# One load of layer 0's projection weights for both token streams, own slots for the first modulation weights, a reordered output projection and new placement spans, in an eight-core diffusion backbone

## The chip, the cores and the metric

The kernel runs on all 8 cores of one Trainium2 chip. Each core works alone on its own batch share (two prompt sequences of 256 tokens and one sample of 1024 tokens); there is no exchange between the cores. The metric is the device time in microseconds (us) of the slowest core.

## What is computed

Four layers, each an attention block and an MLP, are applied to two streams that use the same weights. Per layer `l` and stream:

```
m  = silu(c) @ ada_w[l] + ada_b[l]              # six modulation vectors: sh1 sc1 g1 sh2 sc2 g2
h  = rms_norm(y, norm1_g[l]) * (1 + sc1) + sh1
even l: bg,cg,xa,q,k,v = split(h @ even_w_in)   # 1024 -> 3072
        a   = bg * short_conv(cg * xa)          # width 3 over positions
        att = attention(rms(q), rms(k), v)      # prompt: dense in 256 tokens;
                                                # sample: 2-D neighbourhood + 256 cached keys
odd l:  pooling (short window means) and latent attention (q and kv through low-rank maps)
y += g1 * (concat(a, att) @ w_out)
h  = rms_norm(y, norm2_g[l]) * (1 + sc2) + sh2
y += g2 * (relu(h @ w1)**2 @ w2)                # 1024 -> 4096 -> 1024
```

Outputs are both streams and the prompt's keys, values and latent states of every layer.

## The kernel before, in words

**Layout.** `yT` (float32) and `hT` (bfloat16) hold the 1536 tokens of a core transposed: channels on partitions, tokens in three blocks of 512. Block 0 is the prompt (`GP`, P), blocks 1 and 2 the sample (`GS`, S). All weights lie in device memory as float32 tiles of 128 x 2048 (8 x 256 columns) and are cast to bfloat16 by the DMA that loads them; such a DMA is issued by GpSimd (`wtile`, L813). The page gives its bfloat16 size, 512 KB; 1.05 MB are read. A tile goes into one of the six slots of `WC`, but for the sample's MLP, which has a ring of four slots of its own in the arena (`WB` in `mlp`).

**Stages.** For every layer and stream the program has a group of operations: `aP0` and `aS0` are the attention blocks of prompt and sample in layer 0 (`even_attn`, L1277, or `odd_attn`, L990), `mP0` and `mS0` the MLPs (L894), `adaA` and `adaB` the modulation products (`ada_part`, L839: 8 tiles for shift 1 and scale 1, 16 tiles for the rest). `adaB`'s four closing vector operations wait for all its 16 tiles, and every later update of `yT` reads their result. `norm` (L875) squares 8 chunks of a block on ScalarE, sums them with 8 matmuls against `ones`, takes two ScalarE passes for the reciprocal root (tile `RS`), and then runs 8 pairs of a VectorE product (`NT`) and a shift into `hT`. In an even layer a block's projection is `qk_tile` (L1319), 8 matmuls of 512 columns plus one for the norm, 8 times; `v_tile` (L1348), 16 matmuls of 256 columns, 4 times; and `conv` (L1374), three sets of 8 matmuls of 512 columns, 4 times. `even_attn` loads the 12 tiles of `even_w_in` once for P and once more for S.

`out_proj` (L954) runs weight tile by weight tile: for each of the four tiles both sample blocks are multiplied and added into `yT`; after the last tile come the norms of all blocks. `mlp` starts from these norms.

**Order.** The order on the engines is worked out while the program is built. Every operation has a key. `place` (L219) lays the keys of a group along a span of time, by cumulated TensorE work. `schedule` (L237) then plays the program: at each step the engine that can start first takes, among the operations that can start within 0.12 us (TensorE) or 0.04 us (others), the one with the lowest key. Loads into the same set of slots are issued in the order of their keys, each when a slot is free; a matmul that takes a PSUM bank is held until what its readers need from earlier operations has been placed. The engines then run this fixed order and wait on semaphores. The durations used (in `MMG`, `TRG` and `DMA_RATE`, L216, among others) therefore change the order and nothing else.

The spans (L1514 to L1531) set what runs beside what: the MLP of the prompt beside the sample's attention (`mP` with `aS`), and the prompt's attention of the next layer beside the sample's MLP (`aP` with `mS`). Before, the two of a pair end at the same time.

**Arena.** One piece of SBUF is reused by all stages; a new region waits for every reader and writer of what lay there. In layer 0 the sample takes words 0 to 18496, the prompt 19008 on, and for its V, convolution and probability tiles `BZ` (13056) to 16640.

Of the kernel before, what the change touches and what calls it, by code (L numbers as in the profile page):

```python
# [7 lines left out]
BF16 = mybir.dt.bfloat16  # L8
AF = mybir.ActivationFunctionType
ALU = mybir.AluOpType  # L10
# [102 lines left out]
class Prog:  # L113
# [101 lines left out]
    LAT = {"pe": 0.22, "act": 0.12, "dve": 0.10, "pool": 0.12, "sp": 0.1}  # L215
    DMA_RATE = 0.34e6  # L216
    LEAD = 12.0
# [343 lines left out]
def build(depth=4):  # L561
# [37 lines left out]
    with ExitStack() as st:  # L599
# [30 lines left out]

        SZ, BZ, PZ = 19008, 13056, 4608
        ARENA_W = SZ + PZ
        arena = sb("arena", (128, ARENA_W))
# [75 lines left out]
        def MMG(items, reads, writes, key=None):  # L709
            dur = 0.0  # L710
            fns = []
            for it in items:
                out, lhsT, rhs, start, stop = it[:5]
                skip = len(it) > 5 and it[5]
                n = fsize(rhs)
                dur += max(n / 2400.0 + 0.0025, 0.027) + (0.027 if n <= 128 else 0.0)
                fns.append(lambda h, out=out, lhsT=lhsT, rhs=rhs, start=start, stop=stop, skip=skip:
                           h.matmul(R(out), lhsT=R(lhsT), rhs=R(rhs), start=start, stop=stop, skip_group_check=skip))  # L718
            return P.add("pe", fns, reads, writes, dur, key=key)
# [5 lines left out]
        def TRG(items, reads, writes, key=None):  # L725
            fns = [lambda h, o=o, a=a: h.transpose(R(o), R(a), ident[:, :]) for (o, a) in items]  # L726
            P.add("pe", fns, reads + [bid], writes, 0.085 * len(items), key=key)

# [109 lines left out]

        def ada_part(l, part):  # L839

# [3 lines left out]
            for nt in tiles:  # L844
                w = wtile(WC, ada_w[l, nt])
                its = []
                for j in range(2):
                    c = 2 * (nt * 2 + j - n0)
                    for kc in range(8):
                        its.append((pt[:, c:c + 2], w[:, kc, j * 128:(j + 1) * 128], sTb[:, kc, :], kc == 0, kc == 7))  # L850
                MMG(its, [w.b, bsm], [pt.b])
                P.key += 1
            if part == "A":
                pv = pt[:, 0:32].rearrange("p (n m) -> p n m", m=2)
                for m in range(2):
                    TT(mod[:, l, 0:16, m], pv[:, :, m], adab_sb[:, l, 0:16], ALU.add, [pt.b, bsm], [bmodA[l]])
                for m in range(2):
                    STT(A1[:, l, :, m], mod[:, l, 8:16, m], 1.0, n1g_sb[:, l, :], ALU.add, ALU.mult,
                        [bmodA[l], bsm], [bmodA[l]])
            else:  # L860
                pv = pt[:, 0:64].rearrange("p (n m) -> p n m", m=2)
                for m in range(2):
                    TT(mod[:, l, 16:48, m], pv[:, :, m], adab_sb[:, l, 16:48], ALU.add, [pt.b, bsm], [bmodB[l]])
                for m in range(2):
                    STT(A2[:, l, :, m], mod[:, l, 32:40, m], 1.0, n2g_sb[:, l, :], ALU.add, ALU.mult,
                        [bmodB[l], bsm], [bmodB[l]])

        def grid(ap):
# [85 lines left out]
        def out_proj(G, l, wsrc, lo, blo, hi, bhi, K0, zone):  # L954

            for nq in range(4):
                w = wtile(WC, wsrc[nq], key=K0 + nq * 0.1)
                for k, tb in enumerate(G.tbs):
                    for j in range(2):
# [3 lines left out]
                        prs = [(w[:, kc, j * 128:(j + 1) * 128], lo[:, kc, sl] if kc < 4 else hi[:, kc - 4, sl]) for kc in range(8)]  # L963
                        MMK(pt[:], prs, [w.b] + blo[k] + bhi[k], [pt.b], key=K0 + nq * 0.1)
                        STT(yT[:, n, blk(tb)], pt[:], mod[:, l, 16 + n, G.m:G.m + 1], yT[:, n, blk(tb)],
                            ALU.mult, ALU.add, [pt.b, bmodB[l], by[tb][n]], [by[tb][n]], key=K0 + nq * 0.1)
            for k, tb in enumerate(G.tbs):
                norm(G, l, 2, tb, key=K0 + 1 + k * 0.1, zone=zone)

# [20 lines left out]
        def odd_attn(G, l):  # L990
# [284 lines left out]
            out_proj(G, l, owout[i], poolT, bpool, attT, batt, 40, MM5)  # L1275

        def even_attn(G, l):  # L1277
            i = l // 2
            P.key = 0.0
            S = G.name == "S"  # L1280
# [6 lines left out]
            else:  # L1287
                ar, ax = Arena(SZ, SZ + PZ), Arena(BZ, SZ)
            nv = G.nt + (2 if S else 0)
# [14 lines left out]

            Wt = ewin[i]
            if S:
# [53 lines left out]

            wq = [wtile(WC, Wt[2 + n], key=0.1 + n * 0.02) for n in range(2)]
            wv = [wtile(WC, Wt[n], key=0.11 + n * 0.02) for n in range(2)]
            for k in range(nb):
                P.key = 1 + k * 0.1
                for j in range(4):
                    qk_tile(0, k, j, wq[j // 2])
                    v_tile(k * 4 + j, wv)
            wk = [wtile(WC, Wt[4 + n], key=1.15 + n * 0.02) for n in range(2)]
            for k in range(nb):
# [3 lines left out]

            def conv(j, key):  # L1374
                P.key = key
                wa = wtile(WC, Wt[6 + (j // 2) * 3 + j % 2], key=key - 0.5)
                if j % 2 == 0:
                    wbg[0] = wtile(WC, Wt[6 + (j // 2) * 3 + 2], key=key - 0.4)
                wb = wbg[0]
# [23 lines left out]
            if not S:  # L1403
                for j in range(4):
                    conv(j, 10 + j * 2)
                for h in range(8):
                    j = h // 2
# [18 lines left out]
            for j in range(4):  # L1426
                conv(j, 10 + j * 2.0)
            RG = [(0, 8, 0, 4), (0, 12, 0, 0), (4, 16, 1, 0), (8, 16, 1, 0)]
            kvt = lambda c, b: c // 2 * 4 + b * 2 + c % 2
# [44 lines left out]

        spans = {}

        def group(name, fn, *args):
# [4 lines left out]
        def start():  # L1482
# [10 lines left out]
            TS(cv["gqr"], cv["gqr"], float(96 ** -0.5), None, ALU.mult, None, [bsm], [bsm])  # L1493
            for tb in range(3):
                DMA("sp", [(yT[:, :, blk(tb)], xin[:, tb].rearrange("p (c t) -> p c t", c=8))], [], by[tb], "x%d" % tb, key=-2 + tb)
            ada_part(0, "A")
            LOAD("id", [(ident[:], IDd)], [bid], q="pool", key=20)
# [16 lines left out]
        spans["init"] = (-60.0, 0.0)  # L1514
        spans["nS0"] = (0.0, 30.0)
        spans["aP0"] = (1.0, 110.0)
        spans["adaB0"] = (15.0, 75.0)
        t = 20.0
        for l in range(depth):
            la = P.work("aS%d" % l) + P.work("mP%d" % l) + (75.0 if l == 0 else 0.0)  # L1520
            spans["aS%d" % l] = (t, t + la)
            spans["mP%d" % l] = (max(t, 110.0), t + la)
            spans["adaA%d" % (l + 1)] = (max(t, 110.0), t + 0.7 * la + 30)
            t += la
            lb = P.work("mS%d" % l) + (P.work("aP%d" % (l + 1)) if l + 1 < depth else 0.0)
            spans["mS%d" % l] = (t, t + lb)
            spans["aP%d" % (l + 1)] = (t, t + lb)
            spans["adaB%d" % (l + 1)] = (t, t + 0.5 * lb)
# [117 lines left out]
```

How the kernel before makes its waits and increments, by code:

```python
                def body(h):  # L481
                    for waits, fns, inc, every in lst:
                        for s, v in waits:
                            h.wait_ge(s, v)
                        ins = None
                        for n, fn in enumerate(fns):
                            ins = fn(h)
                            if every:
                                ins.then_inc(inc[0], inc[1])
                        if ins is not None and not every:
                            ins.then_inc(inc[0], inc[1])
```

## Time and profile before

| | us |
|---|---|
| median of 3 runs | 2544.39 |
| lowest and highest of them | 2543.35, 2927.85 |
| profiled execution, its own time | 2548.44 |
| span of its slowest core, core 4 (first to last instruction) | 2546.8 |
| spans of the other cores | 2529.6 to 2545.1 |
| TensorE busy in the span | 2332.6 (92%) |
| VectorE, ScalarE, GpSimd busy | 1172.7, 1165.0, 428.4 |

PE is TensorE's matmuls, PEld its weight loads, DVE VectorE, ACT ScalarE, POOL GpSimd, SP SyncE. PEclk is the granted clock as a share of 2.4 GHz. "DMA share" is the mean busy share of the core's 16 DMA engines. In lists of instructions, the bracket gives the idle time of the engine before the piece and what ended it. Matmuls are pipelined: 64 of them in one piece of 14.19 us is 0.22 us each, although one alone is shown with 0.38 us.

### The profile page before, as it was taken

Reading aid. Unit: us, or ns where it says so; the run is one execution under the profiler, and the core shown is the slowest. Engines: PE = TensorE matmul, PEld = TensorE weight load, DVE = VectorE, ACT = ScalarE, POOL = GpSimd, SP = SyncE. Lnnn points to the kernel's source line nnn. Section 1 sums busy time; section 2 is a strip of 40 time slices with the busy share of each in tenths; the row PEclk is TensorE's granted clock in tenths of the full one; section 3 lists DMA queues with packets and bytes.
Section 4 is the critical chain, followed back from the end, with each engine's and each line's share of the span. In section 5 each row is a group of like instructions: output and inputs, shape, how many; then the busy total and the mean of one; then the engine's idle time right before and its main releaser. Section 6 shows DMA issues by size and latency. Waiting matters only on the chain.

```text
span 2546.8 us, 37971 instructions; the slowest of 8 cores (2529.6 to 2546.8 us)
## 1 busy us (share of the span) xinstructions
PE 2332.6 (92%) x12838; PEld 1120.7 (44%) x13082; DVE 1172.7 (46%) x1819; ACT 1165.0 (46%) x2089; POOL 428.4 (17%) x709
## 2 busy tenths in 40 slices
PE   2868989899998999989999899989999899998999
PEld 1533434345543544334444444444554345343444
DVE  1534445544447423353444645545544663335443
ACT  3535553432517488352232546533443466863111
POOL 3211101212103401021120210122111331000000
PEclk8989999899999999989999899999999999998999
DMA  9998878787542654659845377796755155361444
GB/s 193 150 163 138 154 144 142 121 141 131 92 75 51 112 100 75 99 100 156 143 84 108 61 128 145 141 149 116 134 100 94 21 102 86 56 124 34 75 78 113
DMA packets 97035, 281.87 MB, mean 111 GB/s; under 512 B 18896, under 2 KB 28496, under 8 KB 96848
## 3 DMA queue, kind: packets, MB, share of 16 engines
q0 software_dynamic: 76688, 245.17, 58.7%
q1 hardware_dynamic: 20160, 34.25, 4.3%
q8 instruction: 112, 1.84, 0.3%
q14 instruction: 75, 0.61, 0.1%
HBM read 512.85 MB, written 11.67 MB: 206 GB/s over the span
## 4 chain that ended last, share of the span: by engine, by line
PE 78%; DMA 9%; issue 4%; ACT 3%; DVE 3%; POOL 1%; another core or an unknown queue 0%; DVEq 0%; ACTq 0%; POOLq 0%; SPq 0%
PE psall L718 77%; DMA WC<-ada_w 4%; DMA WC<-even_w_in 2%; ACT arena L742 2%; DMA yT<-xin 2%; DVE NT L764 1%; DMA WC<-mlp_w 1%; ACT RS L742 1%; DMA arena<-rpbx 1%; DVE arena L764 1%; POOL RT L753 1%; PE psall L726 0%; DVE arena L753 0%; ACT hT L742 0%; ACT SQ L742 0%
## 5 line engine op out<-in xcount | busy, mean ns | idle before, releaser
L718 PE MATMUL psall<-arena 128*128 128x512 bf16 (+9 forms) x3818 | 804.5, 353 | 17.8 <-DVE arena L753 4.3
L742 ACT ACTIVATE arena<-psall 128x512 bf16<-128x512 f32 (+6 forms) x747 | 420.5, 584 | 660.4 <-PE psall L718 631.6
L718 PE MATMUL psall<-hT,WC 128*128 128x512 bf16 x2534 | 610.5, 386 | 48.7 <-DMA WC<-even_w_in 11.1
L764 DVE SCALAR_TENSOR_TENSOR yT<-psall,mod,yT 128x512 f32<-128x512 f32 x480 | 359.9, 750 | 494.0 <-PE psall L718 485.5
L718 PEld LDWEIGHTS psall<-arena 128*128 128x128 bf16 (+1 forms) x3896 | 356.0, 98 | 410.5 <-issue 69.8
L718 PE MATMUL psall<-hT,arena 128*128 128x512 bf16 x2025 | 469.0, 384 | 11.1 <-ACT hT L742 5.8
L764 DVE SCALAR_TENSOR_TENSOR arena<-psall,arena 128x512 bf16<-128x512 f32 x384 | 264.5, 690 | 417.2 <-ACT arena L742 413.6
L718 PEld LDWEIGHTS psall<-hT,WC 128*128 128x128 bf16 x2608 | 254.1, 99 | 351.3 <-issue 80.2
L718 PE MATMUL psall<-arena,WC 128*128 128x512 bf16 x1378 | 321.7, 380 | 9.5 <-DVE arena L764 2.9
L718 PEld LDWEIGHTS psall<-hT,arena 128*128 128x128 bf16 x2072 | 203.3, 99 | 251.4 <-issue 23.6
L742 ACT ACTIVATE SQ<-yT 128x512 bf16<-128x512 f32 x192 | 108.2, 618 | 278.0 <-PE psall L718 209.1
L742 ACT ACTIVATE arena<-psall,rkS 128x512 bf16<-128x512 f32 x320 | 195.0, 695 | 41.2 <-PE psall L718 40.4
L718 PEld LDWEIGHTS psall<-arena,WC 128*128 128x128 bf16 x1408 | 136.4, 98 | 173.8 <-issue 15.6
L797 POOL DMA_DIRECT2D arena<-mlp_w x128 | 68.3, 535 | 591.8 <-PE psall L718 577.6
L764 DVE SCALAR_TENSOR_TENSOR NT<-yT,A,RS 128x512 f32<-128x512 f32 x192 | 139.2, 759 | 60.8 <-ACT RS L742 41.9
L797 POOL DMA_DIRECT2D WC<-mlp_w x128 | 68.7, 537 | 579.9 <-PE psall L718 573.1
L718 PE MATMUL psall<-SQ,ones 128*128 128x512 bf16 x211 | 84.0, 476 | 50.0 <-ACT SQ L742 40.6
L742 ACT ACTIVATE RS<-RS 64x512 f32<-64x512 f32 (+1 forms) x180 | 110.3, 624 | 5.6 <-ACT RS L742 0.4
L742 ACT ACTIVATE SQ<-psall 128x512 bf16<-128x512 f32 (+1 forms) x110 | 62.5, 580 | 100.8 <-PE psall L718 100.3
L718 PE MATMUL psall<-WC,hT 128*128 128x256 bf16 (+1 forms) x960 | 104.7, 258 | 3.7 <-DVE arena L753 1.7
L718 PE MATMUL psall<-sTb,WC 128*128 128x2 bf16 x1536 | 52.2, 164 | 57.5 <-DMA WC<-ada_w 57.4
L718 PEld LDWEIGHTS psall<-WC,hT 128*128 128x128 bf16 x960 | 81.9, 99 | 27.6 <-issue 6.6
(81 smaller groups left out, 1177.2 us busy)
## 6 DMA issues: line engine op xcount, KB each, us to landing
WC<-mlp_w POOLq DMA_DIRECT2D x128, 512.0 KB, 6.6
arena<-mlp_w POOLq DMA_DIRECT2D x128, 512.0 KB, 6.1
WC<-ada_w POOLq DMA_DIRECT2D x96, 512.0 KB, 8.3
WC<-even_w_in POOLq DMA_DIRECT2D x48, 512.0 KB, 8.8
arena<-rpbx SPq DMA_DIRECT2D x64, 240.0 KB, 5.2
WC<-even_w_out POOLq DMA_DIRECT2D x16, 512.0 KB, 7.8
WC<-odd_w_in POOLq DMA_DIRECT2D x16, 512.0 KB, 6.4
WC<-odd_w_out POOLq DMA_DIRECT2D x16, 512.0 KB, 6.1
```

What stands on the lines that cost most here:

```text
L718: h.matmul(R(out), lhsT=R(lhsT), rhs=R(rhs), start=start, stop=stop, skip_group_check=skip))
L742: return lambda h: h.activation(out=R(out), in_=R(in_), func=func, **kw)
L753: P.add(eng, [lambda h: h.tensor_tensor(out=R(out), in0=R(in0), in1=R(in1), op=op)], reads, writes, vdur(fsize(out), eng, isb(out, in0, in ...
L764: P.add("dve", [lambda h: h.scalar_tensor_tensor(out=R(out), in0=R(in0), scalar=scalar, in1=R(in1), op0=op0, op1=op1)], reads, writes, vdu ...
L797: fns = [lambda h, o=o, i_=i_: h.dma_start(out=R(o), in_=R(i_)) for (o, i_) in pairs]
```

## The change

Five edits, in one diff:

1. In layer 0 the 12 tiles of `even_w_in` are loaded once. `wt` keeps the tile of the prompt's call and hands it to the sample's; it stays in its `WC` slot until both have used it. The two projections get one common span, the convolutions (`cP0`, `cS0`) and the rest (`hP0`, `hS0`) groups of their own. The prompt's V, convolution and probability tiles begin at word 14592 (`JZ`).
2. The first 8 modulation tiles go to 8 slots of their own in the arena. The first x block is loaded at once, the second when the fourth modulation tile has landed, the third when the sixth has.
3. `out_proj` holds its four tiles and runs block by block, each block followed by its own norm, in every layer.
4. New spans: the prompt's MLP ends at 0.9 of the sample's attention (1.05 in the last layer), the prompt's attention at 0.85 of the sample's MLP.
5. The planner's model: a DMA rate of 0.30 in place of 0.34 MB per us, no extra 0.027 us for matmuls of at most 128 columns, 0.056 in place of 0.085 us for a transpose.

```diff
-    DMA_RATE = 0.34e6
+    DMA_RATE = 0.30e6
...
+        JZ = 14592
...
-                dur += max(n / 2400.0 + 0.0025, 0.027) + (0.027 if n <= 128 else 0.0)
+                dur += max(n / 2400.0 + 0.0025, 0.027)
...
-            P.add("pe", fns, reads + [bid], writes, 0.085 * len(items), key=key)
+            P.add("pe", fns, reads + [bid], writes, 0.056 * len(items), key=key)
...
-        def ada_part(l, part):
+        def ada_part(l, part, res=None):
+            loads = []
...
-                w = wtile(WC, ada_w[l, nt])
+                w = wtile(res or WC, ada_w[l, nt])
+                loads.append(w)
...
-            for nq in range(4):
-                w = wtile(WC, wsrc[nq], key=K0 + nq * 0.1)
-                for k, tb in enumerate(G.tbs):
+            ws = [wtile(WC, wsrc[nq], key=K0 + nq * 0.1) for nq in range(4)]
+            for k, tb in enumerate(G.tbs):
+                for nq in range(4):
+                    w = ws[nq]
...
-            for k, tb in enumerate(G.tbs):
-                norm(G, l, 2, tb, key=K0 + 1 + k * 0.1, zone=zone)
+                norm(G, l, 2, tb, key=K0 + k * 0.5 + 0.45, zone=zone)
...
+        shared = {}
+
         def even_attn(G, l):
             i = l // 2
+            joint = l == 0
+
+            def wt(n, key):
+                if not joint:
+                    return wtile(WC, ewin[i, n], key=key)
+                if n not in shared:
+                    shared[n] = wtile(WC, ewin[i, n], key=key)
+                return shared[n]
...
-                ar, ax = Arena(SZ, SZ + PZ), Arena(BZ, SZ)
+                ar, ax = Arena(SZ, SZ + PZ), Arena(JZ if joint else BZ, SZ)
...
             def conv(j, key):
+                if joint:
+                    P.grp = "c" + n_ + "0"
...
+                if joint:
+                    P.grp = "hP0"
...
+            if joint:
+                P.grp = "hS0"
...
+        PE1, PE2, PE3 = 0.9, 0.85, 1.05
...
+            xload(0, [])
+            AR = Arena(4096, SZ).ring(8, (128, 8, 256), BF16, "WA")
+            wA = ada_part(0, "A", AR)
+            xload(1, [wA[3].b])
+            xload(2, [wA[5].b])
...
-        spans["nS0"] = (0.0, 30.0)
-        spans["aP0"] = (1.0, 110.0)
-        spans["adaB0"] = (15.0, 75.0)
-        t = 20.0
+        spans["nS0"] = (1.0, 10.0)
+        qkv = P.work("aP0") + P.work("aS0")
+        cnv = P.work("cP0") + P.work("cS0")
+        spans["aP0"] = spans["aS0"] = (0.0, qkv)
+        spans["cP0"] = (qkv, qkv + 25)
+        spans["cS0"] = (qkv, qkv + cnv + 20)
+        spans["hP0"] = (qkv, qkv + cnv)
+        spans["adaB0"] = (10.0, qkv + cnv)
+        t = qkv + cnv
         for l in range(depth):
-            la = P.work("aS%d" % l) + P.work("mP%d" % l) + (75.0 if l == 0 else 0.0)
-            spans["aS%d" % l] = (t, t + la)
-            spans["mP%d" % l] = (max(t, 110.0), t + la)
-            spans["adaA%d" % (l + 1)] = (max(t, 110.0), t + 0.7 * la + 30)
+            n = "hS0" if l == 0 else "aS%d" % l
+            la = P.work(n) + P.work("mP%d" % l)
+            spans[n] = (t if l else qkv + 30, t + la)
+            spans["mP%d" % l] = (t, t + la * (PE1 if l + 1 < depth else PE3))
+            spans["adaA%d" % (l + 1)] = (t, t + 0.7 * la)
             t += la
             lb = P.work("mS%d" % l) + (P.work("aP%d" % (l + 1)) if l + 1 < depth else 0.0)
             spans["mS%d" % l] = (t, t + lb)
-            spans["aP%d" % (l + 1)] = (t, t + lb)
+            spans["aP%d" % (l + 1)] = (t, t + lb * PE2)
```

## Rows read from the trace of the kernel before

**Rows 1.** The profile page: busy time, DMA queues, chain by engine.

```profile
PE 2332.6 (92%) x12838; PEld 1120.7 (44%) x13082; DVE 1172.7 (46%) x1819; ACT 1165.0 (46%) x2089; POOL 428.4 (17%) x709
...
PE 78%; DMA 9%; issue 4%; ACT 3%; DVE 3%; POOL 1%; another core or an unknown queue 0%; DVEq 0%; ACTq 0%; POOLq 0%; SPq 0%
```

**Rows 2.** Busy time by stretch; the last three columns are PEclk, DMA share, GB/s.

```profile
0.00:500.00 500.00, 393.21 (x2341) 191.76 (x2383) 220.79 (x373) 231.87 (x418) 97.53 (x153) 0.91 0.89 153
500.00:2547.00 2047.00, 1939.43 (x10499) 928.90 (x10700) 951.88 (x1447) 933.16 (x1672) 330.88 (x556) 0.97 0.57 100
...
0.00:60.00 60.00, 15.00 (x151) 6.42 (x152) 6.04 (x17) 19.33 (x33) 24.07 (x29) 0.82 0.97 197
60.00:200.00 140.00, 101.26 (x758) 58.30 (x771) 67.97 (x116) 67.40 (x114) 24.84 (x43) 0.87 0.96 156
200.00:469.00 269.00, 252.58 (x1282) 117.31 (x1307) 129.50 (x215) 124.61 (x235) 39.62 (x69) 0.98 0.85 146
```

**Rows 3.** Waits, 60 to 200 us: total us, times, longest.

```profile
POOL WC L797 <- PE psall L718: 84.0, 30, 8.2
...
PE psall L718 <- DMA WC<-ada_w: 17.4, 9, 3.6
PE psall L718 <- DMA WC<-even_w_in: 12.6, 9, 3.7
```

**Rows 4.** DMA, 0 to 500 us: the GpSimd queue; then issues, 60 to 200 us.

```profile
q0 software_dynamic: 19680, 59.68, 77.5%
...
WC<-even_w_in POOLq DMA_DIRECT2D x14, 512.0 KB, 13.2
WC<-ada_w POOLq DMA_DIRECT2D x14, 512.0 KB, 10.6
WC<-even_w_out POOLq DMA_DIRECT2D x4, 512.0 KB, 14.8
```

**Rows 5.** The start: chain, then instructions of PE in order of time.

```profile
1.99 39.86 DMA yT<-xin
...
56.11 0.19 DVE mod L753
...
53.68 2.32 PE L718 MATMUL psall<-sTb,WC 128*128 128x2 bf16 x80
65.42 3.19 PE L718 MATMUL psall<-hT,WC 128*128 128x512 bf16 x7 [9.42 <-ACT RS L742]
```

**Rows 6.** PE in order of time around one end of the sample's attention.

```profile
1689.67 14.19 PE L718 MATMUL psall<-arena,WC 128*128 128x512 bf16 x64
...
1721.57 3.80 PE L718 MATMUL psall<-hT,arena 128*128 128x512 bf16 x10 [1.03 <-ACT RS L742]
```

**Rows 7.** Busy time by stretch, at the seven stage boundaries; columns as in rows 2.

```profile
469.00:491.00 22.00, 15.58 (x114) 5.83 (x115) 9.79 (x16) 15.47 (x28) 5.78 (x10) 0.64 0.94 140
1084.00:1106.00 22.00, 12.83 (x109) 5.30 (x110) 10.94 (x18) 15.67 (x28) 5.44 (x9) 0.63 0.77 134
1703.00:1722.00 19.00, 12.16 (x109) 5.08 (x109) 8.56 (x13) 14.40 (x27) 5.53 (x9) 0.71 0.90 159
2302.00:2320.00 18.00, 9.50 (x26) 2.69 (x25) 11.03 (x17) 13.74 (x23) 2.10 (x2) 0.67 0.00 0
773.00:802.00 29.00, 20.02 (x111) 8.55 (x114) 25.35 (x38) 23.48 (x47) 13.34 (x18) 0.88 0.08 16
1402.00:1419.00 17.00, 12.19 (x38) 4.70 (x40) 11.30 (x17) 11.54 (x21) 6.72 (x7) 0.60 0.45 48
2004.00:2018.00 14.00, 7.70 (x24) 2.66 (x24) 12.94 (x19) 10.86 (x21) 5.92 (x7) 0.64 0.01 2
```

**Rows 8.** ACT and DVE in order of time at 1084 us: pieces of one norm.

```profile
1085.29 4.99 ACT L742 ACTIVATE SQ<-yT 128x512 bf16<-128x512 f32 x9 [33.27 <-PE psall L718]
...
1092.93 1.41 DVE L764 SCALAR_TENSOR_TENSOR NT<-yT,A,RS 128x512 f32<-128x512 f32 x2 [7.10 <-ACT RS L742]
```

**Rows 9.** Busy time, 900 to 1050 us: the sample's attention of layer 1.

```profile
900.00:1050.00 150.00, 140.52 (x729) 60.82 (x742) 45.63 (x69) 122.01 (x209) 17.20 (x27) 0.98 0.52 87
```

More of the change, by code:

```diff
@@ L866, in ada_part @@
                         [bmodB[l], bsm], [bmodB[l]])
+            return loads
         def grid(ap):
@@ L963, in out_proj @@
                         prs = [(w[:, kc, j * 128:(j + 1) * 128], lo[:, kc, sl] if kc < 4 else hi[:, kc - 4, sl]) for kc in range(8)]
-                        MMK(pt[:], prs, [w.b] + blo[k] + bhi[k], [pt.b], key=K0 + nq * 0.1)
+                        MMK(pt[:], prs, [w.b] + blo[k] + bhi[k], [pt.b], key=K0 + k * 0.5 + nq * 0.1)
                         STT(yT[:, n, blk(tb)], pt[:], mod[:, l, 16 + n, G.m:G.m + 1], yT[:, n, blk(tb)],
-                            ALU.mult, ALU.add, [pt.b, bmodB[l], by[tb][n]], [by[tb][n]], key=K0 + nq * 0.1)
-            for k, tb in enumerate(G.tbs):
-                norm(G, l, 2, tb, key=K0 + 1 + k * 0.1, zone=zone)
+                            ALU.mult, ALU.add, [pt.b, bmodB[l], by[tb][n]], [by[tb][n]], key=K0 + k * 0.5 + nq * 0.1)
+                norm(G, l, 2, tb, key=K0 + k * 0.5 + 0.45, zone=zone)
         def values(ar, nv):
@@ L1303, in even_attn @@
             z0 = ar.off
-            Wt = ewin[i]
             if S:
@@ L1359, in v_tile @@
                     STORE(G, [(nav_out[i, vt * 128:(vt + 1) * 128, :], o[:])], [o.b])
-            wq = [wtile(WC, Wt[2 + n], key=0.1 + n * 0.02) for n in range(2)]
-            wv = [wtile(WC, Wt[n], key=0.11 + n * 0.02) for n in range(2)]
+            wq = [wt(2 + n, 0.1 + n * 0.02) for n in range(2)]
+            wv = [wt(n, 0.11 + n * 0.02) for n in range(2)]
             for k in range(nb):
@@ L1367, in even_attn @@
                     v_tile(k * 4 + j, wv)
-            wk = [wtile(WC, Wt[4 + n], key=1.15 + n * 0.02) for n in range(2)]
+            wk = [wt(4 + n, 1.15 + n * 0.02) for n in range(2)]
             for k in range(nb):
@@ L1374, in conv @@
             def conv(j, key):
+                if joint:
+                    P.grp = "c" + n_ + "0"
                 P.key = key
-                wa = wtile(WC, Wt[6 + (j // 2) * 3 + j % 2], key=key - 0.5)
+                wa = wt(6 + (j // 2) * 3 + j % 2, key - 0.5)
                 if j % 2 == 0:
-                    wbg[0] = wtile(WC, Wt[6 + (j // 2) * 3 + 2], key=key - 0.4)
+                    wbg[0] = wt(6 + (j // 2) * 3 + 2, key - 0.4)
                 wb = wbg[0]
@@ L1493, in start, with xload @@
             TS(cv["gqr"], cv["gqr"], float(96 ** -0.5), None, ALU.mult, None, [bsm], [bsm])
-            for tb in range(3):
-                DMA("sp", [(yT[:, :, blk(tb)], xin[:, tb].rearrange("p (c t) -> p c t", c=8))], [], by[tb], "x%d" % tb, key=-2 + tb)
-            ada_part(0, "A")
+            def xload(tb, after):
+                DMA("sp", [(yT[:, :, blk(tb)], xin[:, tb].rearrange("p (c t) -> p c t", c=8))], after, by[tb], "x%d" % tb, key=-2 + tb)
+            xload(0, [])
[3 more added lines that the diff above has]
+            xload(2, [wA[5].b])
             LOAD("id", [(ident[:], IDd)], [bid], q="pool", key=20)
```

## The prediction, made before the changed kernel ran

> **What bounds the kernel now.** I read the page first. TensorE is busy for 2332.6 of 2546.8 us and has 78% of the chain, no other engine more than 3% of it [rows 1]. So the question is only where TensorE stands still or runs slowly: 214 us without a matmul, and busy time at a granted clock below 1. The other engines matter where TensorE waits for them.
>
> Second, the busy time by stretch [rows 2]. Up to 500 us TensorE is busy for 393.2 us, at a mean clock of 0.91; behind that for 1939.4 of 2047 us, at 0.97. Half of the idle time lies in the first fifth, and the DMA engines are 89% busy there, 96% from 60 to 200 us, against 57% later. Third, the waits of that stretch [rows 3]: TensorE waits 17.4 and 12.6 us for weight tiles, and GpSimd, which issues their loads, stands 84.0 us because all slots of `WC` still belong to matmuls that have not run. The opening is thus bound by DMA and slots together. Fourth, the order of PE's instructions where the stretches show a low clock later [rows 6, 7]: these are the seven places where one stage of the sample ends and the next waits for its norm. At 1703.7 us the last `out_proj` matmul is done and the MLP's first comes at 1721.6; between them stand only norm sums and a few modulation products (109 matmuls), and the clock falls to 0.71 over the stretch.
>
> All sums below are against the profiled execution, 2548.4 us (span 2546.8, 1.6 around it). It lies 4 us above the median of the runs, 2544.4, and I take these 4 us off at the end.
>
> **Part 1, layer 0's tiles loaded once (edit 1) and the start (edit 2): 55 us, between 20 and 75.** Worked out from both sides.
>
> By DMA. The GpSimd queue moved 59.68 MB in 77.5% of 500 us [rows 4], 154 MB per ms of full work, so one tile of 0.524 MB costs 3.4 us of all 16 engines. Twelve tiles fewer are 41 us of DMA work; at the share of 0.89 that the stretch reached [rows 2] they are 46 us of time, if the stretch stays bound by DMA as before.
>
> By TensorE. Busy time by clock gives the work at full clock: 393.2 x 0.91 = 358 us up to 500, of which 15.0 x 0.82 = 12 us are done by 60 us. The other 346 need, at the pace of 200 to 469 us (252.6 x 0.98 / 269 = 0.92 [rows 2]), 376 us. They start when the prompt's first projection can: now at 65.4 us [rows 5], behind the three x blocks (landed after 39.9 us), the modulation (56.1) and the prompt's norm. With the x blocks staggered and no slot to wait for, the modulation needs eight tiles (27 us), x block 0 and what the others take in between. By size and the same rate the three blocks (2.1 MB each) ended at 42 with six or seven tiles: 8 tiles and 3 blocks are then about 49 us at worst, against 56.1, so the first projection comes at about 58. 58 + 376 = 434: 66 us less than 500. If TensorE ran at 0.94 instead, it would be 75.
>
> I take 55, between the 46 by DMA and the 66 by TensorE, since both sides have to be served: the new order gives TensorE three blocks' work for each tile (three times the load: 8 matmuls of 0.22 us for each of two halves of the tile and three blocks are 10.6 us against 3.4), but 0.89 of DMA share cannot rise far. The lower bound 20 is that only the tiles loaded twice up to 200 us count (four at the start and 14 from 60 us on [rows 4], less the prompt's 12: 6 tiles, 3.4 us each), the rest being hidden under the stretch behind it. These 55 hold the first of the boundaries by 9 us; it is counted there, not here, so part 1 alone is 46.
>
> The Trainium skill ("DMA: Bandwidth & Descriptors", Specifications) gives a core some 358 GB/s from device memory; since a tile is read as float32, 1.05 MB, that is 2.9 us a tile, an estimate from that page. By it the twelve tiles would be worth 35 us of DMA work, and the forecast 7 us later. The trace has 3.4, with which I reckon.
>
> What the joint load adds: the sample's matmuls of q, k, v and the convolutions read tiles that stay in the six slots for longer, while 16 `adaB` tiles and four output tiles of the prompt must pass through what is left; that is the slow rival below. `JZ` puts the prompt's V and probability tiles under the sample's probability and bias buffers, so no head of the sample starts before the prompt's attention is done; the cover is 62 us of convolution matmuls, which wait for none of this, so I price it at nothing (5 us of ScalarE's start if the cover is short).
>
> **Part 2, `out_proj` by block (edit 3): 36 us, between 12 and 45.** The cost of the four boundaries behind the sample's attention is the stretch less busy time by clock [rows 7]: 22 - 15.6 x 0.64 = 12.0; 22 - 12.8 x 0.63 = 13.9; 19 - 12.2 x 0.71 = 10.4; 18 - 9.5 x 0.67 = 11.6; together 47.9. Now the first block's norm runs under the second block's 64 matmuls (half of the 128 of both blocks; 64 take 14.2 us [rows 6]). A norm is 8 squares (4.99 us for nine), two passes over `RS` and 8 products (1.41 us for two [rows 8]): some 13 us. The first norm is then hidden. The second starts where both started before, but the MLP's first four tiles have 64 matmuls for block one, again 14 us against 13. The loads of these tiles are in the ring `WB`, on ground that the attention has left. I leave 3 us a boundary (the order has to be found by the planner, and the products share VectorE with the `yT` updates, 0.75 us each) and get 9 each, 36. If the MLP found no matmul that can run before the second norm, the second norm would stay bare and a third be saved per boundary, 12 or so in all; full removal is 45.
>
> The Trainium skill ("TensorE: Matmul & The Clock Gate", HAM oscillation) says that a TensorE that waits between short bursts falls back to half clock and pays again. The trace agrees: 0.63 to 0.71 at these stretches, 1.2 GHz for a part of each. It gives no further term, as busy time by clock holds it.
>
> **Part 3, the prompt placed ahead (edit 4): 15 us, between 0 and 27.** At the three boundaries behind the sample's MLP the cost is 29 - 20.0 x 0.88 = 11.4; 17 - 12.2 x 0.60 = 9.7; 14 - 7.7 x 0.64 = 9.1; together 30.2 [rows 7]. With the prompt's attention done at 0.85 of the stage, its MLP for the next layer can run there. But its loads share the order of `WC` with the sample's new projection, so one or two tiles will be there, 3.5 us of matmuls each: half, 15. `adaB` waits stay.
>
> **Part 4, what the edits give back: 8 us, between 0 and 25.** The sample's attention keeps ScalarE 81% busy while TensorE has 0.94 [rows 9], with the prompt's MLP as filler. That MLP now ends at 0.9 of the stage. `out_proj` begins at about 0.86 of it, so little attention is left bare; and four of six `WC` slots are held through `out_proj`, so the filler behind it comes late. 2 to 3 us in each of three stages. Edit 5 changes only the order; 0, within 5 either way, as its numbers come closer to the trace (0.034 us per two-column matmul: 80 in 2.32 less the tail [rows 5]; 1.05 MB in 3.4 us is 0.31 MB per us).
>
> **Sum.** 46 + 36 + 15 - 8 = 89. 2548.4 - 89 = 2459.4; less the 4 us, **2455**.
>
> **The rivals.**
>
> *The opening gives little (2486).* GpSimd's 84 us of waiting for slots [rows 3] may remain the limit, as tiles are held longer. Then part 1 is worth 20 at most, part 3 10: 20 + 36 + 10 - 8 = 58, and 2544 - 58 = 2486; with a half of part 2, 2504. For it: loads that landed 10.6 to 14.8 us behind their issue [rows 4]. Against it: each tile brings three blocks' work.
>
> *Everything is filled (2409).* Part 1 by TensorE, 66, or 75 with the first boundary; part 2 behind that 33, part 3 27, part 4 nothing: 135, so 2409. For it: only TensorE's own work is left then, and the clock holds 1.00 wherever it is fed. Against it: DMA would have to work at 0.95 and more for 400 us.
>
> *Slots starve TensorE (slower, 2584).* Place: `WC` between the first projection and the sample's last convolution. 16 `adaB` tiles and 4 output tiles must pass. With a single free slot each costs its landing, its issue (0.5) and its matmuls (0.5, or 3.5 for an output tile): 16 x (10.6 + 1.0) + 4 x (14.8 + 4.0) = 261 us [rows 4]. The cover is projections and convolutions of three blocks: 72 matmuls of 0.22 us and 64 of 0.11 make 23 us a block, 96 of 0.22 make 21, so 132 for three. 129 us are missing, and 2455 + 129 = 2584. It decides, against the 89 us gained, from 132 + 89 = 221 us on, or 11 us a tile; two slots in turn would halve the price and cost nothing. Against it: four of six slots are held in the first half, so two rotate.
>
> *The change doesn't do what it says (2544).* The planner's order could undo it: the closing products of `adaB` gate all `yT` updates, and with `adaB` stretched to the end of the convolutions the prompt's MLP starts later. What part 1 brings is lost at 200 to 450 us, where 0.85 of the DMA are busy. With part 2 at its lower end this is 2544 - 12 - 8 = 2524 to 2544.
>
> **How the numbers follow.** Forecast 0.50 (2430 to 2480), little from the opening 0.22, everything filled 0.15, undone 0.09, starved 0.04. What a measurement of this kernel can tell from no change is about 2%, 51 us, so faster means below 2493.5. The forecast, all of the filled case and three quarters of the second are faster: 0.50 + 0.15 + 0.17 = 0.82. Slower than 2595 is the upper half of the starved case and a little for what I don't see, 0.03; the same has the other 0.15. The range: from the filled case, 2405, to 2512 in the second, which leaves some 0.05 below and 0.14 above.
>
> **What would show it.** `even_w_in` loads are 36 in place of 48; the first projection comes at about 58 us and TensorE is over 90% busy from 60 to 200 (101 of 140 now). The 393 us of busy work are done by about 445. At the four attention boundaries norm sums stand between `psall<-arena,WC` or `hT,WC` matmuls, and the gap to the first MLP matmul is under 5 us at a clock near 1. At the MLP's end prompt matmuls stand among the norm sums. It is wrong if DMA share from 60 to 450 stays at 0.9 while TensorE idles as before, if GpSimd's waits at `WC` grow and TensorE waits over 30 us for `ada_w` or `even_w_out`, or if the gaps move from the boundaries into the attention stages.

## The result, and the profile after

The changed kernel takes 2443.2 us (median of 4 runs, 2437.7 to 2445.4). The ratio to the kernel before is 0.9595, with a 95% interval of 0.9571 to 0.9619: 4% faster. Forecast were 2455 in a range of 2405 to 2512. The ratios are formed from undisturbed executions alone. Where a time in us is given for an experiment below, it is the ratio times 2544, if it is not called a median.

The profile page of the changed kernel, the rows that answer to [rows 1]:

```profile
span 2443.9 us, 38189 instructions; the slowest of 8 cores (2428.3 to 2443.9 us)
...
PE 2311.9 (95%) x13082; PEld 1117.5 (46%) x13082; DVE 1165.8 (48%) x1815; ACT 1184.9 (48%) x2115; POOL 400.1 (16%) x675
...
PE 84%; DMA 8%; issue 2%; ACT 2%; DVE 1%; POOL 1%; DVEq 0%; ACTq 0%; POOLq 0%; SPq 0%
```

TensorE's work is the same, the time around it is less. I count as lost what a stretch has beyond its busy time by clock, as in the prediction. The clock comes rounded to two digits and from one execution on one core, so a difference of a few us over a long stretch says nothing. Busy time by stretch, the columns as in [rows 2]:

```profile
0.00:60.00 60.00, 17.48 (x188) 10.53 (x189) 11.69 (x24) 17.54 (x28) 20.44 (x27) 1.00 0.98 193
60.00:200.00 140.00, 120.49 (x792) 65.21 (x791) 76.75 (x127) 81.42 (x140) 23.26 (x33) 0.90 0.60 104
200.00:469.00 269.00, 245.72 (x1342) 114.02 (x1341) 129.65 (x219) 129.13 (x241) 44.69 (x77) 0.94 0.88 156
...
500.00:2444.00 1944.00, 1897.28 (x10525) 912.52 (x10522) 928.41 (x1420) 940.35 (x1680) 298.26 (x519) 0.99 0.59 105
```

Up to 500 us the kernel before had done 393.2 x 0.91 = 358 us of full-clock work [rows 2]. The changed kernel has done 17.5 + 108.4 + 231.0 = 357 by 469 us. The opening with the first boundary gave 31 us; the other 72 of the 103 us between the spans came behind it.

The stretches of the seven boundaries, of the same lengths as in [rows 7], four behind the sample's attention and three behind its MLP:

```profile
450.00:472.00 22.00, 22.00 (x146) 10.65 (x145) 10.06 (x14) 12.05 (x22) 5.25 (x8) 1.00 0.85 135
1042.00:1064.00 22.00, 21.06 (x142) 11.22 (x141) 17.94 (x28) 16.22 (x27) 6.00 (x9) 1.00 0.83 141
1625.00:1644.00 19.00, 16.34 (x101) 7.26 (x99) 14.62 (x23) 11.99 (x22) 5.70 (x8) 0.82 0.59 108
2200.00:2218.00 18.00, 18.00 (x86) 8.13 (x83) 9.61 (x15) 7.76 (x13) 0.00 (x0) 1.00 0.20 66
745.00:774.00 29.00, 26.20 (x173) 12.58 (x171) 16.24 (x28) 19.52 (x37) 10.01 (x14) 1.00 0.33 56
1348.00:1365.00 17.00, 17.00 (x109) 9.43 (x108) 12.68 (x20) 12.88 (x22) 8.56 (x9) 1.00 0.62 79
1920.00:1934.00 14.00, 12.39 (x88) 6.02 (x87) 10.35 (x16) 9.81 (x19) 7.25 (x12) 1.00 0.22 37
```

The first four lose 0 + 0.9 + 5.6 + 0 = 6.5 us in place of 47.9. The last three lose 2.8 + 0 + 1.6 = 4.4 in place of 30.2. How such a place looks now, PE in order of time (the answer to [rows 6], at the last one): norm sums stand between projection matmuls (`arena,WC`) and the MLP's first (`hT,arena`).

```profile
2209.36 1.03 PE L719 MATMUL psall<-SQ,ones 128*128 128x512 bf16 x4
2210.23 1.89 PE L719 MATMUL psall<-hT,arena 128*128 128x512 bf16 x8
2211.95 1.03 PE L719 MATMUL psall<-SQ,ones 128*128 128x512 bf16 x4
2212.82 1.89 PE L719 MATMUL psall<-arena,WC 128*128 128x512 bf16 x8
```

In the opening something new is seen. PE in order of time, then the ScalarE piece that belongs to it:

```profile
50.28 3.57 PE L719 MATMUL psall<-hT,WC 128*128 128x512 bf16 x8 [8.79 <-ACT hT L743]
...
74.56 1.63 PE L719 MATMUL psall<-SQ,ones 128*128 128x512 bf16 x3 [4.60 <-ACT SQ L743]
...
89.89 0.57 PE L719 MATMUL psall<-sTb,WC 128*128 128x2 bf16 x16 [6.72 <-DMA WC<-ada_w]
94.10 3.57 PE L719 MATMUL psall<-hT,WC 128*128 128x512 bf16 x8 [3.65 <-ACT hT L743]
...
73.79 1.67 ACT L743 ACTIVATE SQ<-yT 128x512 bf16<-128x512 f32 x3 [2.02 <-DMA yT<-xin]
```

The first projection comes at 50.3 us, 15 earlier than before [rows 5]. But at 70 the prompt's share is done, and the sample's projection starts only at 94. The last x block has landed only at 73.8. In the kernel before it was issued at 2.6 us and landed 45.0 us later, at about 48:

```profile
yT<-xin SPq DMA_DIRECT2D x1, 2048.0 KB, 45.0
```

And while TensorE waits, little is loaded: the DMA share from 60 to 200 us fell from 0.96 to 0.60. GpSimd has filled all six slots of `WC` by 22 us and then issues no further weight tile until 69.5, which is the wait of 47.1 us in this list (the waits of 60 to 200 us, against [rows 3]):

```profile
POOL WC L798 <- PE psall L719: 125.9, 17, 47.1
...
PE psall L719 <- DMA WC<-ada_w: 7.4, 2, 6.7
```

### The profile page after: what moved, and what is told of

Same layout as the page of the kernel before. It is cut to its first block, busy times and chain, and to the rows that moved or that the text cites. A ratio compares the mean times of both kernels' runs of the same rounds, so it can differ in the third digit from the quotient of the medians.

```text
span 2443.9 us, 38189 instructions; the slowest of 8 cores (2428.3 to 2443.9 us)
## 1 busy us (share of the span) xinstructions
PE 2311.9 (95%) x13082; PEld 1117.5 (46%) x13082; DVE 1165.8 (48%) x1815; ACT 1184.9 (48%) x2115; POOL 400.1 (16%) x675
## 4 chain that ended last, share of the span: by engine, by line
PE 84%; DMA 8%; issue 2%; ACT 2%; DVE 1%; POOL 1%; DVEq 0%; ACTq 0%; POOLq 0%; SPq 0%
PE psall L719 84%; DMA WC<-ada_w 2%; DMA arena<-rpbx 2%; DMA arena<-ada_w 1%; DMA WC<-mlp_w 1%; DMA nav_out<-NT 1%; ACT arena L743 1%; ACT RS L743 1%; DMA arena<-mlp_w 1%; DVE NT L765 0%; PE psall L727 0%; POOL RT L754 0%; ACT hT L743 0%; DVE arena L765 0%; POOL hT L788 0%
## 5 line engine op out<-in xcount | busy, mean ns | idle before, releaser
L719 PE MATMUL psall<-arena 128*128 128x512 bf16 (+8 forms) x3896 | 814.5, 353 | 24.9 <-ACT arena L743 8.6
L743 ACT ACTIVATE arena<-psall 128x512 bf16<-128x512 f32 (+4 forms) x745 | 416.7, 579 | 671.6 <-PE psall L719 654.2
L743 ACT ACTIVATE hT<-NT,mod 128x512 bf16<-128x512 f32 x133 | 93.2, 721 | 47.2 <-DVE NT L765 46.0
L765 DVE SCALAR_TENSOR_TENSOR arena<-psall,cst,RS 64x256 bf16<-64x256 f32 (+2 forms) x122 | 73.7, 608 | 46.3 <-ACT RS L743 43.3
L719 PE MATMUL psall<-SQ,ones 128*128 128x512 bf16 x222 | 68.9, 401 | 25.4 <-ACT SQ L743 23.6
```

The source lines that it names most:

```text
L743: return lambda h: h.activation(out=R(out), in_=R(in_), func=func, **kw)
L765: P.add("dve", [lambda h: h.scalar_tensor_tensor(out=R(out), in0=R(in0), scalar=scalar, in1=R(in1), op0=op0, op1=op1)], reads, writes, vdu ...
```

## The experiments

Twelve kernels ran. Seven are one edit away from the changed kernel (2443 us), and three are two edits away from it: the old start with store tiles and the two gated ones. The last two are one edit away from the kernel before (2544 us).

**The output projection as before.** `out_proj` got its old body back (the lines with a minus in its part of the diff above, and their keys); norms of all blocks at the end.

> The changed kernel with the output projection run tile by tile as before and all norms at its end; everything else stays. Theory A (the norm behind the projection was bare, and running block by block hides it at all four ends of the sample's attention): 36 us slower than the changed kernel's 2443, so about 2480, and the stretches of norm sums at a low clock are back at four places. Theory B (with the prompt's stages placed ahead, the prompt's next attention fills that place anyway): within 12 us, 2443 to 2455.

Measured: ratio 0.9746 (0.9723 to 0.9770), 2479 us: 38 slower than the changed kernel. Theory A holds for the time, B falls. Busy time of this kernel at its four boundaries:

```profile
460.00:480.00 20.00, 15.27 (x115) 6.12 (x113) 11.54 (x17) 15.75 (x29) 7.78 (x10) 0.71 0.85 142
1080.00:1100.00 20.00, 12.59 (x92) 6.04 (x91) 7.52 (x12) 5.46 (x11) 3.32 (x6) 0.74 1.04 203
1655.00:1680.00 25.00, 20.47 (x212) 10.89 (x209) 19.79 (x29) 18.82 (x33) 9.95 (x16) 1.00 1.04 160
2240.00:2260.00 20.00, 13.87 (x53) 5.52 (x51) 15.10 (x23) 12.26 (x20) 3.15 (x3) 0.83 0.14 53
```

They lose 9.2, 10.7, 4.5 and 8.5 us. At three of the four the low clock is back, and the prompt's work placed ahead did not fill them. At the third it did: the clock stays at 1.00, and 4.5 us are lost, no more than the 5.6 of the changed kernel there. So theory A's "four places" are three. The four rows lose 33 us, the changed kernel 6.5 at these places: that is 26 of the 38 us, and the rest is not located.

**The prompt's stages spread to the end again.**

```diff
-        PE1, PE2, PE3 = 0.9, 0.85, 1.05
+        PE1, PE2, PE3 = 1.0, 1.0, 1.0
```

> The changed kernel with the prompt's stages spread to the end of the sample's again (all three factors 1.0). Theory A (the prompt ahead is what fills the three ends of the sample's MLP): 25 to 30 us slower, about 2470, with gaps before the sample's next projection. Theory B (the new durations in the planner's model and the block-wise projection do it, the factors little): within 10 us.

Measured: 0.9768 (0.9751 to 0.9785), 2485 us: 44 slower, more than even theory A had. The place is the one it named, but wider than I had cut it. The end of the sample's MLP with the projection behind it, first the kernel before, second the changed one, third this experiment:

```profile
765.00:885.00 120.00, 103.05 (x682) 53.00 (x692) 74.58 (x119) 75.78 (x150) 46.55 (x77) 0.96 0.48 80
1398.00:1498.00 100.00, 84.59 (x445) 41.46 (x452) 52.05 (x86) 48.99 (x82) 20.02 (x26) 0.90 0.51 80
2000.00:2110.00 110.00, 94.32 (x584) 47.78 (x594) 73.55 (x119) 69.74 (x140) 46.47 (x75) 0.95 0.40 69
```

```profile
737.00:857.00 120.00, 110.92 (x761) 57.93 (x759) 73.47 (x121) 67.88 (x135) 40.15 (x71) 1.00 0.51 86
1340.00:1440.00 100.00, 98.02 (x573) 50.94 (x571) 55.01 (x89) 52.73 (x88) 18.64 (x28) 1.00 0.64 104
1915.00:2025.00 110.00, 103.14 (x699) 56.91 (x698) 63.47 (x105) 66.28 (x135) 37.66 (x69) 1.00 0.47 80
```

```profile
745.00:865.00 120.00, 106.10 (x718) 54.81 (x717) 74.20 (x119) 71.01 (x144) 50.46 (x82) 0.94 0.48 82
1360.00:1460.00 100.00, 90.18 (x493) 44.74 (x490) 54.94 (x90) 52.62 (x88) 20.77 (x29) 0.91 0.57 89
1940.00:2050.00 110.00, 95.88 (x602) 48.74 (x601) 74.60 (x121) 69.97 (x141) 44.65 (x72) 0.97 0.38 64
```

Three rows each, by stretch: lost are 21.1 + 23.9 + 20.4 = 65 us before, 9.1 + 2.0 + 6.9 = 18 in the changed kernel, and 20.3 + 17.9 + 17.0 = 55 here. So 37 of the 44 us lie at these three places. The run puts all three factors back together, so it does not say what each is worth.

**The sample loads its projection tiles again.**

```diff
-                if not joint:
+                if True:
                     return wtile(WC, ewin[i, n], key=key)
```

> The changed kernel, but the sample loads its twelve projection tiles of layer 0 once more, 36 to 48 loads of even_w_in. Theory A (the opening is bound by the amount of DMA work): 41 us of DMA work more, 40 to 46 us slower, about 2487. Theory B (the opening is bound by slots and by the order, the DMA engines are only 0.60 busy from 60 to 200 us now): 10 to 25 us slower, since part of the loads falls into idle DMA time.

Measured: 0.9681 (0.9662 to 0.9700), 22 us slower, in the range of theory B. Its stretch of 60 to 200 us:

```profile
60.00:200.00 140.00, 104.00 (x710) 57.57 (x709) 66.54 (x107) 78.93 (x134) 22.48 (x36) 0.88 0.78 132
```

The DMA share rises from 0.60 to 0.78. That is 25 us of DMA work more in this stretch, so more than half of the 41 us of loads falls into time in which the DMA engines stood still.

**The old start.** The first modulation tiles in the common slots, no staggering.

```diff
-            AR = Arena(4096, SZ).ring(8, (128, 8, 256), BF16, "WA")
-            wA = ada_part(0, "A", AR)
-            xload(1, [wA[3].b])
-            xload(2, [wA[5].b])
+            xload(1, [])
+            xload(2, [])
+            ada_part(0, "A")
```

> The changed kernel with the first eight modulation tiles in the common slots and all three x blocks loaded at once, as before. Theory A (own slots and staggered x blocks bring the prompt's first projection from 65 to 50 us, and this comes through): 12 to 15 us slower, about 2457. Theory B (the prompt's early start is lost again at 70 to 94 us, where the sample's norm waits): within 5 us.

Measured: 2428.6 us (median; 2427.3 to 2435.2), ratio 0.9554 (0.9533 to 0.9574). Neither theory: this kernel is faster than the changed one, by 10 us in the ratio and 15 in the medians. The intervals just overlap, the runs do not (2437.7 to 2445.4 there). First projection and first stretches of this kernel:

```profile
65.86 2.82 PE L719 MATMUL psall<-hT,WC 128*128 128x512 bf16 x7 [9.40 <-ACT RS L743]
```

```profile
0.00:60.00 60.00, 14.81 (x151) 6.47 (x152) 5.59 (x16) 19.26 (x33) 24.60 (x30) 0.81 0.96 195
60.00:200.00 140.00, 130.63 (x878) 73.53 (x895) 85.27 (x136) 83.54 (x144) 21.75 (x34) 0.97 0.72 117
```

TensorE starts 15 us later and then hardly stops: 48.0 + 13.3 = 61 us lost by 200 us, against 42.5 + 31.6 = 74 in the changed kernel. The next runs ask why.

**Store tiles of their own.** The prompt's value tiles go to two buffers in the arena in place of `NT`, which the norms share; in the profile of the changed kernel `NT` waits 11.1 us for `nav_out` between 60 and 200 us.

```diff
+            VO = [] if S else [ar.ring(1, (128, 512), F32, "voa"), ax.ring(1, (128, 512), F32, "vob")]
...
-                    o = Tl(P, NT)
+                    o = Tl(P, VO[vt % 2])
```

> The changed kernel, but the prompt's four value tiles of an even layer are stored from two tiles of their own and no longer from the two slots of NT, which the norms need. Theory A (the stores, 10 to 15 us each behind queued weight tiles, hold both NT slots and so the sample's norm at 61 to 92 us): the gap of 20 us before the sample's first projection closes, 12 to 20 us faster than the changed kernel, about 2427, and the wait of NT for nav_out is gone. Theory B (the second and third x block come too late for that norm anyway): within 5 us of 2443.

Measured: 0.9595 (0.9580 to 0.9609), the changed kernel's ratio. Theory A has the place right and the time wrong. The wait for the stores is gone, and the sample's projection comes at 79.6 us in place of 94.1, so it was the stores that had held it. But TensorE then waits 8 us for a modulation tile, as this kernel's order of PE shows, and nothing is gained:

```profile
79.56 3.57 PE L719 MATMUL psall<-hT,WC 128*128 128x512 bf16 x8 [9.64 <-ACT hT L743]
...
107.68 0.56 PE L719 MATMUL psall<-sTb,WC 128*128 128x2 bf16 x16 [8.02 <-DMA WC<-ada_w]
```

**Old start and store tiles.**

> Old start (modulation tiles in the common slots, all x blocks at once) and store tiles of their own together. If the stores are what the new start ran into (theory A), the old start has little of that wait (1 us), so the two together are at 2428, as the old start alone, and the new start with store tiles beats or equals it. If it is the x blocks (theory B), this stays at 2428 and the new start with store tiles at 2443.

Measured: 0.9551 (0.9532 to 0.9570), as the old start alone. The stores cost nothing there either. With store tiles in both, the intervals of old start and new start (0.9580 to 0.9609) no longer overlap: the old start is faster, by 11 us.

**All x blocks at once, own slots kept.** `xload(1, [])` and `xload(2, [])`.

> The changed kernel with own slots for the modulation tiles, but all three x blocks loaded at once. Theory A (stores): the blocks are there by 45 us, the sample's norm can run before the stores take the NT slots; most of the gap at 70 to 94 us closes, about 2430. Theory B' (not the x blocks but the order in which matmuls wait for modulation tiles behind full slots costs the time): 2443, with TensorE still waiting for ada_w there.

Measured: 0.9640 (0.9626 to 0.9654), 2452 us: 11 slower than the changed kernel, which neither theory had. Against the old start, which also loads all x blocks at once, it is 22 us slower: that is what the own slots cost by themselves, and staggering the x blocks wins back half of it. Its PE in order of time:

```profile
56.77 2.67 PE L719 MATMUL psall<-SQ,ones 128*128 128x512 bf16 x5 [25.18 <-ACT SQ L743]
73.06 2.67 PE L719 MATMUL psall<-SQ,ones 128*128 128x512 bf16 x5 [11.91 <-ACT SQ L743]
88.19 3.57 PE L719 MATMUL psall<-hT,WC 128*128 128x512 bf16 x8 [9.03 <-ACT hT L743]
```

Issued by 2.6 us, the second and third x block land only at 56 and 72 us. In the old start they landed at 43 and 48. The issue of the third block in the DMA view (the last number is the us from issue to landing), first the old start, then this kernel:

```profile
yT<-xin SPq DMA_DIRECT2D x1, 2048.0 KB, 45.7
yT<-xin SPq DMA_DIRECT2D x1, 2048.0 KB, 69.6
```

The difference is what else is under way: 14 weight tiles (8 modulation, 4 projection, 2 more modulation) in place of 7. And TensorE, which runs its order as it was planned, stands behind the sum of squares of blocks that have not come.

**The projection tiles gated.** As the last, and the first four projection tiles wait for the third x block; in a second kernel for the second.

```diff
+                    shared[n] = wtile(WC, ewin[i, n], key=key, after=by[2] if n < 4 else [])
```

> Own slots for the eight modulation tiles, all x blocks loaded at once, and the first four projection tiles issued only when the third x block has landed, so that only modulation tiles and x are under way before. Theory B (what costs the new start its 15 us is that more weight tiles are queued early and the x blocks of the sample land at 57 and 73 us in place of 42): x has landed by about 50 us, the first projection comes at 55 to 60 us and goes on without a gap; 2418 to 2428, at least 15 us under the same kernel without the gate (2453). Theory C (own slots are bad for another reason, the planner's order): stays at 2440 to 2453.

> As the run with the gate on the third x block, but with the gate on the second. By theory B the four tiles then again share the DMA engines with the third x block, which lands some 10 us later; the first projection a little earlier: between 2420 and 2440, not under the other gate by more than 5.

Measured: 0.9568 (0.9551 to 0.9585) and 0.9574 (0.9559 to 0.9590), 2434 and 2436 us, 18 and 17 faster than without the gate. That confirms the mechanism of theory B, and not its size: with the first gate the third block now lands at 54 us (50.9 from its issue), but the prompt's first projection comes at 70.6, and 2418 to 2428 is missed by 6 us.

```profile
48.50 2.67 PE L719 MATMUL psall<-SQ,ones 128*128 128x512 bf16 x5 [16.35 <-ACT SQ L743]
55.05 2.66 PE L719 MATMUL psall<-SQ,ones 128*128 128x512 bf16 x5 [2.17 <-ACT SQ L743]
70.55 3.57 PE L719 MATMUL psall<-hT,WC 128*128 128x512 bf16 x8 [9.03 <-ACT hT L743]
```

With the second gate the third block lands at 55.5, hardly later and not by 10 us, and the first projection comes at 72.2, later and not earlier. The squares of both sample blocks stand ahead of the last modulation matmuls in the order, so the prompt waits for them too. An order that takes the prompt's norm first with x blocks that land early was not tried.

**The planner's old durations.** The three numbers of edit 5 back.

> The changed kernel with the planner's old durations. Theory A (they change only the order and little of it): within 5 us of 2443. Theory B (part of the 75 us gained behind the opening is due to them, as the waits for weight tiles at 1450 to 1485 us are gone): 10 to 20 us slower, with waits for mlp_w and ada_w of TensorE back at the start of layer 2.

Measured: 0.9704 (0.9688 to 0.9720), 28 us slower, more than theory B had. Busy time of this kernel over the opening, then behind the MLPs:

```profile
0.00:60.00 60.00, 14.48 (x169) 8.30 (x170) 11.18 (x23) 16.32 (x25) 20.45 (x27) 1.00 0.97 191
60.00:200.00 140.00, 119.86 (x803) 66.22 (x802) 73.02 (x119) 86.01 (x147) 19.35 (x29) 0.91 0.63 105
200.00:469.00 269.00, 240.03 (x1271) 109.80 (x1270) 127.43 (x218) 120.81 (x226) 41.44 (x72) 0.94 0.87 149
747.00:867.00 120.00, 108.93 (x723) 54.87 (x722) 71.23 (x117) 70.18 (x137) 38.40 (x70) 0.96 0.56 89
1356.00:1456.00 100.00, 95.85 (x562) 50.12 (x561) 52.13 (x85) 52.17 (x86) 17.67 (x26) 1.00 0.59 95
1938.00:2048.00 110.00, 102.97 (x683) 56.63 (x681) 61.80 (x105) 67.00 (x131) 37.99 (x68) 0.98 0.42 71
```

It loses 15.4 + 4.2 + 9.1 = 29 us at the three MLP ends, 11 more than the changed kernel. By 469 us it has done 14.5 + 109.1 + 225.6 = 349 us of full-clock work, 8 less than the changed kernel. Where the other 9 lie is open. The waits for tiles that theory B named did not all come back: behind 450 us TensorE waits 3.5 us for `mlp_w` and 6.9 for `ada_w`, against 2.2 and 4.7 in the changed kernel.

**Two edits alone, in the kernel before.** The block-wise projection; the planner's new durations.

> The kernel before with the block-wise output projection alone. Theory A (the edit stands by itself): 27 to 40 us faster than before, 2505 to 2517, the same 36 to 38 as were lost by taking it out of the changed kernel. Theory B (it needs the new placement around it): under 15 us.

> The kernel before with the planner's new durations alone. Taking them out of the changed kernel cost about 25 us. Theory A (they order the loads nearer to when they land, in any kernel): 15 to 25 us faster than before, about 2525. Theory B (they matter only together with the new spans, which are laid out in the model's own TensorE time): within 8 us.

Measured: 0.9832 (0.9815 to 0.9850), 43 us faster, and 0.9929 (0.9908 to 0.9951), 18 faster. The projection needs nothing around it and gives even a little more than theory A had. The durations help in either kernel.

## Why the prediction was right, point by point

The time and the direction were right, 12 us from the median. That it came so close is luck in part: the opening gave 27 us less than forecast (19 in place of 46), the ends of the sample's MLP 32 more (47 in place of 15), and the two errors cancel. Edit 5, which was put at nothing, is hidden inside both.

**Part 2, the block-wise projection: right.** Forecast were 36 us, 9 for each boundary. The stretches lose 6.5 in place of 47.9, a gain of 41; taking the edit out costs 38, putting it alone into the kernel before gives 43. The mechanism was the one named: at these places norm sums now stand among matmuls of the projection and of the MLP.

**Part 1, opening: the size failed, and so did the reason for it.** The step was "they are 46 us of time, if the stretch stays bound by DMA as before". It did not stay so: with tiles held for both streams the DMA share from 60 to 200 us went to 0.60. I had that slot limit as a rival ("the opening gives little") with 20 us for part 1. Measured are 31 us up to the point that was 500 us before, of which 12 are the first boundary: 19. The edits in it pull apart. The shared tiles are worth 22 (taken out alone), the new start costs 10 to 15, and the planner's new durations bring 8 of their 28 here: 22 - 10 + 8 = 20.

I had credited the new start with an early projection, and the projection did come at 50 us, 8 earlier than I reckoned. TensorE was then to be over 90% busy from 60 to 200 us; it is 86%, and GpSimd's waits for slots of `WC` grew from 84.0 to 125.9 us, which the prediction had named as a sign of being wrong. Two things were wrong in the reckoning of the x blocks. The landing at 42 us (39.9 from issue, [rows 5]) that I took for all three is that of the second; the third landed at 48, so "49 us at worst" was too early, and the gated kernel, which has just eight tiles beside the three blocks, has the third at 54. And I left out the six further tiles that are issued from 8.8 to 21 us, since slots of `WC` are free. With all x blocks loaded at once they move the third block from 54 to 72 us, and the gate, which takes them away, gives 18 us: that part is shown. In the changed kernel itself, where the blocks are staggered, the same six tiles also fill `WC` until 69.5 us, so that no load follows; what each of the two costs there is not separated. Nor is the rest of the new start's cost: the gated kernel is still 4 us (ratio, with overlapping intervals) behind the old start. Its third block lands 5 us later than there and its first projection comes 5 us later, but by 200 us it has lost 56 us, no more than the 61 of the old start.

The Trainium skill ("DMA: Bandwidth & Descriptors", Queues, rings and completion order) says that each DMA engine takes turns between the queues that have work. The trace agrees in kind, as neither queue goes first: beside fourteen tiles the first two blocks land at 27 and 56 us, ahead of some of the tiles, of which the last land at about 66, and the third block behind them all, at 72. Beside eight tiles the third lands at 54. That is 19 us for six tiles; with the 3.4 us a tile of the prediction it is 20, an estimate.

**Part 3, the prompt ahead: mechanism right, term too small.** Forecast 15 us from 30; measured 44 by taking the factors out. The mis-sized step was the stretch: I priced the norm's gap, stretches of 14 to 29 us that lose 30 together, and not the projection behind it, in which TensorE also runs out of matmuls: the stretches of 100 to 120 us lose 65. "One or two tiles" of filler was too few as well: over the long stretches 47 of the 65 us are gone. That the prompt's earlier placement fills them is shown by the run without the factors, where 37 of these 47 come back. The other changes of the spans in edit 4 were not taken out by themselves.

**Part 4, give-back: not seen.** I expected 8 us in the attention stages. The gains at the boundaries (41 and 47) and in the opening (19 beside its boundary) add up to 107, the spans differ by 103: what was given back elsewhere is 4 us by this count, and none of the runs isolates it.

**Edit 5: called nothing, worth 18 alone and 28 on top.** The step "changes only the order; 0, within 5 either way" took it for small because its numbers are small. But the planner decides with them at every step which load goes out when. The figure beside it was misread, too: 80 matmuls in 2.32 us [rows 5] are 0.029 us each, and 0.027 without the last one's tail, not 0.034.

The terms as measured one by one, 22 - 10 + 38 + 44 + 28 = 122, are more than the 101 us of the whole: some places are filled by more than one edit, as the MLP ends by the factors and the durations.

The rivals: starved slots and the undone change did not come, and neither did "everything is filled" (its 66 us for the opening already held the first boundary; the 75 belong to a pace of 0.94); "little from the opening" was right about the opening and wrong about the sum, as its remaining terms were the small ones.

Against both kernels, the old start with the rest of the change is the fastest version that ran: 2428.6 us, ratio 0.9554.

## What to carry to other kernels

Where stages follow each other on a bound engine, look at a stretch well past the visible gap: the ramp of the next stage may cost more than the gap. Reorder the last product of a stage by block so that its norm runs under the next block, before looking for foreign work to fill. And a load that is needed early can be delayed by the loads that free slots let out beside it; here more slots made the start worse.

## What the runs showed of the hardware

Three x blocks of 2 MB, issued on SyncE's queue in the first 3 us, landed at 26, 43 and 48 us beside seven casting weight tiles on GpSimd's queue, at 27, 48 and 54 us beside eight, and at 27, 56 and 72 us beside fourteen. The first block hardly notices what is queued beside it, the last one comes later with every tile.
